# The three sums that fold a modulation block's slabs: made by VectorE behind the third chunk of a body, not by GpSimd

## What is computed

```
for l in range(DEPTH):                       # DEPTH = 2
    mods = split(silu(c) @ w_ada[l] + b_ada[l], 9)          # c: one vector; also for c_ctx
    h = post_norm(h, 0.5*mods[2] * swiglu(modulate(h, mods[0], mods[1]), ffn1_up[l], ffn1_down[l]), ...)
    y = token_mixer(modulate(h, mods[3], mods[4]), ...)     # convolution, mLSTM, differential attention
    h = post_norm(h, mods[5] * y, ...)
    h = post_norm(h, 0.5*mods[8] * swiglu(modulate(h, mods[6], mods[7]), ffn2_up[l], ffn2_down[l]), ...)
    # the same for the context tokens hc with mods_c, but for the end of the last layer
```

## Time and profile before

| | |
|---|---|
| time, median of 3 runs | 2405.98 us (2404.79 to 2406.38) |
| the profiled execution, time | 2403.49 us |
| its span in the trace | 2401.5 us |
| TensorE busy, share of the span | 98% |
| VectorE busy | 66% |
| ScalarE busy | 42% |
| GpSimd busy | 7% |
| granted TensorE clock, mean | 0.998 of full speed |

### The profile page before, as it was taken

How to read it: one execution, slowest core, us unless ns; L and a number is a source line. 1 busy time by engine, 2 the same in 40 slices (tenths; PEclk the granted TensorE clock), 3 DMA queues, 4 the chain that set the end, 5 groups by cost and what they waited for, 6 DMA issues and landing times.

```text
span 2401.5 us, 35644 instructions
## 1 busy us (share of the span) xinstructions
PE 2362.2 (98%) x13050; PEld 2034.4 (85%) x13050; DVE 1586.5 (66%) x2616; ACT 1003.3 (42%) x1666; POOL 175.9 (7%) x168
## 2 busy tenths in 40 slices
PE   7999999999999999999999999999999999999998
PEld 4888888887888778898888898888898898998998
DVE  6898577445546555568885368886666556667875
ACT  6432224434335334363222254322255456555554
POOL 0111010000000000021111000111100000001220
PEclk9999999999999999999999999999999999999999
DMA  8687464232222322327773327775534333556654
GB/s 277 214 253 246 122 211 132 80 93 74 62 65 77 97 79 62 114 76 238 247 242 118 97 79 242 240 236 178 167 95 126 107 102 101 163 146 180 192 158 133
DMA packets 557847, 355.31 MB, mean 148 GB/s; under 512 B 15078, under 2 KB 515344, under 8 KB 557712
## 3 DMA queue, kind: packets, MB, share of 16 engines
q1 hardware_dynamic: 556264, 353.13, 49.4%
q10 hardware_dynamic: 1448, 0.38, 0.1%
HBM read 335.63 MB, written 17.83 MB: 147 GB/s over the span
## 4 chain that ended last, share of the span: by engine, by line
PE 90%; DVE 3%; ACT 3%; issue 2%; DMA 2%; SPq 1%; POOL 0%; DVEq 0%; ACTq 0%; POOLq 0%
PE ps L938 26%; PE ps L940 26%; PE ps L939 26%; PE ps L1223 2%; PE ps L1021 1%; PE ps L1022 1%; PE ps L1023 1%; PE ps L1238 1%; PE ps L1199 1%; PE ps L1255 1%; DMA raw<-in_ffn_up 1%; SPq L718 1%; DVE w_lo L1964 1%; ACT w_hi L1362 1%; PE ps L1169 0%
## 5 line engine op out<-in xcount | busy, mean ns | idle before, releaser
L938 PE MATMUL ps<-u_hi,w_hi 128*128 128x512 f32 (+2 forms) x2368 | 859.5, 363 | 1.3 <-DVE scr L2282 1.1
L940 PE MATMUL ps<-u_hi,w_lo 128*128 128x512 f32 (+2 forms) x2368 | 848.4, 358 | 0.0
L939 PE MATMUL ps<-u_lo,w_hi 128*128 128x512 f32 (+2 forms) x2368 | 847.9, 358 | 0.0
L1964 DVE TENSOR_TENSOR w_lo<-raw,w_hi 128x1024 fp32r<-128x1024 f32 (+3 forms) x432 | 497.6, 1153 | 513.5 <-ACT w_hi L1362 511.4
L1362 ACT ACTIVATE w_hi<-raw 128x1024 fp32r<-128x1024 f32 (+3 forms) x432 | 425.4, 985 | 915.4 <-PE ps L940 818.4
L938 PEld LDWEIGHTS ps<-u_hi,w_hi 128*128 128x128 f32 x2368 | 447.3, 189 | 66.2 <-DVE scr L2282 1.3
L940 PEld LDWEIGHTS ps<-u_hi,w_lo 128*128 128x128 f32 x2368 | 447.1, 189 | 65.9
L939 PEld LDWEIGHTS ps<-u_lo,w_hi 128*128 128x128 f32 x2368 | 447.5, 189 | 62.7
L2345 DVE SCALAR_TENSOR_TENSOR ada_acc<-ada_in_up,cs,ada_acc 128x512 f32<-128x512 f32 x378 | 273.2, 786 | 0.2 <-DMA ada_in_up<-in_w_ada 0.2
L938 PE MATMUL ps<-g_hi,w_hi 128*128 128x512 f32 (+1 forms) x704 | 244.3, 347 | 1.3 <-DVE scr L2302 1.3
L940 PE MATMUL ps<-g_hi,w_lo 128*128 128x512 f32 (+1 forms) x704 | 241.5, 343 | 0.0
(11 more groups left out here) (299 smaller groups left out, 2974.8 us busy)
## 6 DMA issues: line engine op xcount, KB each, us to landing
raw<-in_ffn_up SPq DMA_DIRECT2D x152, 512.0 KB, 4.0
raw<-in_w_in SPq DMA_DIRECT2D x132, 512.0 KB, 3.6
ada_in_up<-in_w_ada SPq DMA_DIRECT2D x108, 512.0 KB, 4.3
raw<-in_ffn_down SPq DMA_DIRECT2D x67, 384.0 KB, 3.5
fold_out<-ada_acc SPq DMA_DIRECT2D x32, 512.0 KB, 3.0
fold<-fold_out SPq DMA_DIRECT2D x32, 512.0 KB, 5.3
raw<-in_ffn_down SPq DMA_DIRECT2D x42, 320.0 KB, 3.3
h<-in_ffn_up SPq DMA_DIRECT2D x22, 512.0 KB, 3.8
```

Of the source, the lines that this page charges most:

```text
L938: pe.matmul(ps[bank][:, cols_of], wh, a_hi, start=a, stop=False)
L939: pe.matmul(ps[bank][:, cols_of], wh, a_lo, start=False, stop=False)
L940: m = pe.matmul(ps[bank][:, cols_of], wl, a_hi, start=False, stop=b)
L1964: dve.tensor_tensor(lo, whole, hi.bitcast(F32), ALU.subtract).then_inc(lo_done, 1)
```

## The change

GpSimd's `fold_sums` goes. The same three sums, with the same waits, become instructions of VectorE. In an up stage they stand behind q = 2 of the body whose end transposes the block. In a down stage they stand behind the `w_lo` of q = 0. Nothing is changed on TensorE, ScalarE or SP, nor in the sizes.

```
-        def fold_sums(first, count):                       # GpSimd
-            for block in range(first, first + count):
-                pool.wait_ge(fold_landed, 16 * (block - 3))
-                for step, n in enumerate((4, 2)):
-                    pool.tensor_tensor(fold[:, 0:n, :], fold[:, 0:n, :], fold[:, n:2 * n, :], ALU.add
-                                       ).then_inc(fold_half, 1)
-                    pool.wait_ge(fold_half, 2 * (block - 4) + step + 1)
-                pool.tensor_tensor(fold[:, 0, :], fold[:, 0, :], fold[:, 1, :], ALU.add).then_inc(fold_done, 1)
...
-            fold_sums(ADA_OF[layer, "up0"], ADA_UP)
-            fold_sums(ADA_OF[layer, "down0"], ADA_DOWN[layer])
...
-            if layer == 0:
-                fold_sums(ADA_OF[0, "up1"], ADA_UP)
...
+        def fold_sums(block):                              # VectorE
+            dve.wait_ge(fold_landed, 16 * (block - 3))
+            for step, n in enumerate((4, 2)):
+                dve.tensor_tensor(fold[:, 0:n, :], fold[:, 0:n, :], fold[:, n:2 * n, :], ALU.add).then_inc(fold_half, 1)
+                dve.wait_ge(fold_half, 2 * (block - 4) + step + 1)
+            dve.tensor_tensor(fold[:, 0, :], fold[:, 0, :], fold[:, 1, :], ALU.add).then_inc(fold_done, 1)
...
             # up, body(i), end of the loop over q
+                    if q == 2 and add:
+                        fold_sums(block - begin + i)
...
             # down, body(i)
                     ahead(base, q, i, 8, down_kn(q))
+                    if q == 0 and block is not None and 0 < i <= ADA_DOWN[layer]:
+                        fold_sums(block + i - 1)
...
             # down, last body
             ahead(base, 0, i, 8, down_kn(0, two))
+            if block is not None and i <= ADA_DOWN[layer]:
+                fold_sums(block + i - 1)
             centre(n, (0, 1, 2, 3))
```

## The result

The changed kernel took 2456.41 us (median of 5 runs, 2455.97 to 2458.77), the kernel before 2405.98 beside it: ratio 1.0215 [1.0203, 1.0226], 50.4 us slower. The prediction was 2449.5 within 2438 to 2466. It holds; its largest term was too small all the same, and that is what the experiments are about.

The account below looks back on a forecast made before the run. TensorE, 90% of the span, was taken to bound the kernel. Steady waits 34.5, first-body pause 6.05, clock 1.7 and down stages 1.3 sum to 43.6 us, giving 2449.5 us, range 2438 to 2466.

Parts of the forecast that it names:

- So only what makes TensorE wait counts.: Whole kernel: TensorE is 90% of the span, GpSimd 0%; the change could win only about 1 us, 0.04%.
- The chain of 6.84 us: Steady up body: from chunk 2's end through high half, low half, four products and sums, against TensorE's 5.48 us of work.
- The restart 0.15: TensorE after a wait: 0.15 us to resume, added to 1.36 of waiting in each steady up body.
- the steady term: Up bodies with adds and products: 23 waits of 1.5 us each, 34.5 us; bounds 1.1 and 2.1 a wait.
- The ninth add: Up-stage body that adds without products: 4.15 us of work against 5.48, so TensorE does not wait.
- Body 1: First up stage, where VectorE is late: sums done at 97.12, one longer TensorE pause, +6.05 us once.
- The clock: After the first up stage's long pause TensorE's granted clock could fall: +1.7 us, bounds 0 and 3.4.
- Down stages: Middle bodies hide the sums; the last body's sums and centring come later: +1.3 us, between 1.1 and 1.6.
- The faster adder wins: VectorE takes up the sums at their landing and both pauses on GpSimd go: 2404.9 us, not slower; 5%.
- Only the stage's start is late: TensorE's pause at the up stage's start lets VectorE catch up for good: 12 us, 2418 us; 7%.
- VectorE becomes the bound: Low-half delays meet late loads; 23 up bodies stretch by 3 us each: 2484 us; 6%.
- The rule weighed against it: VectorE's elementwise adds are about twice as fast and GpSimd's slow its products: by this alone, free or a small gain.

Follow-up runs that it names:

- the second profile: The changed kernel run once more with nothing altered, beside the one with block 4's sums on GpSimd: 2457.91 us, 1.0218 against the kernel before.
- alone: Against the kernel before, only the down stages' five sets of sums moved to VectorE, the up stages' 27 left on GpSimd: 2406.6 us, ratio 1.0007.
- the mixture above: Against the kernel before, up-stage sums on VectorE ahead of chunk q = 2's low half; block 4 and down stages stay on GpSimd: 2405.59 us, 1.0001.

## Why the prediction was right, point by point

- **"So only what makes TensorE wait counts."** Right. Each kernel's time follows from its pauses, how long they are and where they stand.
- **The chain of 6.84 us.** Right. It put the sums 1.36 late; they were 1.27 late. The sums by themselves, from rows of other lines of VectorE, were priced 1.52 and took 1.46 (217.45 to 218.91).
- **"The restart 0.15", the term that was mis-sized.** "I take 1.5" a body became 1.91 in the mean. The 0.15 came from one pause in body 1, outside the loop, where the product is 0.10 behind the transpose. Behind 18 of the 23 pauses stands the loop's jump back, with 0.58. The restart is 0.14 + 0.58 there, less the 0.03 of an undisturbed body: 0.69 instead of 0.15. I had named the loop's wait only as a reason to double the restart in the upper bound (2.1 a body, which still covers it). So the steady term was too small: 34.5 forecast, 44.0 measured, and writing out the loop took 11.3 away. The other terms missed by less: +1.7 in body 1, -0.3 and -0.8 for the clock and the down stage. The bodies that pause are 23, as this sum has it, not the 24 of the forecast's last paragraph.
- **"The ninth add ... no wait."** Right: 4.15 us of chain against 5.48 of cover, and no pause in any of the three.
- **Body 1, "+6.05".** It was +7.77. The links behind ScalarE's high half took 98.83 - 93.57 = 5.26 against 5.35 forecast. But ScalarE's load let it start 1.89 later than in the trace of before (92.48 against 90.59), and VectorE, which I had put there at 91.61, was free 0.30 before its low half, at 93.27, since its first products had waited for a store until 84.95. TensorE itself was ready 1.01 later (91.63 against 90.62), so the pause grew less than the shift. In the second profile the sums end at 97.35, 0.23 from my 97.12, and the transpose is 6.29 later than before. I had carried the times of a load and a store over from a single execution; with the sums on GpSimd that body's pause ranges from 0.34 to 1.14 over the profiles, and with the changed kernel it is 7.10 and 6.83.
- **The clock, "+1.7".** 1.40 in one profile, 25.99 - 23.52 = 2.5 in the other. Inside its bounds.
- **Down stages, "+1.3".** 0.54 in one profile, 1.38 (28.98 - 27.60) in the other and 1.30 alone. Right in kind; the sums start on the landing of a load that varies by a microsecond.
- **The rivals.** *The faster adder wins* was out: VectorE is the faster adder, 1.46 us against 3.30, and it does not reach the work in time. *Only the stage's start is late* fell with the steady pauses. *VectorE becomes the bound* fell too: no body's pause grows from one to the next, and ScalarE's high half is 0.3 us behind TensorE still.
- **The rule weighed against it.** The rows agree with what it says: the sums are twice as fast on VectorE, and products beside GpSimd's adds were slower (3.93 for four, now 2.73). The Trainium skill (GPSIMD Engine Reference, sections 4.1 and 8) gives both. What decided is the queue that the sums join, and the mixture above shows that the gain, taken without the pauses, is not to be told from 0 (1.0001 [0.9992, 1.001]).

## What to carry to other kernels

Before work moves to a faster engine, sum up what stands ahead of it in that engine's program since the last thing it waits for, and set that against the cover of the engine that waits for the result: here 6.84 us against 5.48, and with the four products moved behind the sums 44 of the 50 us were gone. A lateness repeats in every body when the late chain itself starts from the engine that it holds up. And leave room: with TensorE's wait at the end of its loop, a result that came just in time cost 0.65 us a body.

## What was unexpected of the hardware

- **A jump back of TensorE's hardware loop right behind a late wait** put the next product matmul 0.58 us behind the transpose, against 0.36 where the loop is left, 0.29 where it is entered, 0.12 in straight code (body 1) or 0.10 with no loop at all, and 0.02 where nothing was late. It is paid when no idle time is shown ahead of the transpose too (22.57 against 22.00 us a body, the sums 0.04 us ahead). How far ahead they must be, between 0.13 and 1.4 us, was not tried. What in the jump takes the time no run shows.
- **The clock falls after short pauses.** With pauses of 1.09 to 1.25 us between stretches of 22 us of matmuls the granted clock stayed at 1.00; with 1.69 to 1.86 us it fell in 8 of 23 bodies (0.93 over the one shown), each 1.6 us longer. So 0.6 us more of pause cost on average some 1.15 us a body, not 0.6 (27.6 / 24).
